# A two-block network on one Trainium2 core: the first mixer reordered, its rotation done by VectorE, and six modulation chunks summed by VectorE within the attention steps

## The reference, cut to what matters

```
mod = (silu(c) @ ada_w[layer] + ada_b[layer])      # 1024 -> 6144, for 2 layers
sh1, sc1, g1, sh2, sc2, g2 = split(mod, 6)
h = rms_norm(x, norm1_g) * (1 + sc1) + sh1
rq, rk, rv, rg, aq, ak, av = split(h @ w_in)       # 1024 -> 3584
rq, rk = rotary(rq), rotary(rk) * RET_DIM ** -0.5  # x1*cos - x2*sin, x1*sin + x2*cos
ret = head_rms(retention(rq, rk, rv)) * silu(rg)
att = chunk_attention(rms_norm(aq), rms_norm(ak), av, rel_bias)   # 8 heads of 64
x = x + g1 * (concat([ret, att]) @ w_out)
```

## Time and profile before

| | us |
|---|---|
| three runs, median | 1947.06 |
| profiled execution | 1949.58 |
| its span in the trace | 1947.8 |
| TensorE busy in it | 1744.1 |
| VectorE busy in it | 1256.5 |

### The profile page before, as it was taken

One profiled execution on the slowest core, in us unless ns is written; L12 is line 12 of the kernel. 1 busy time (PEld: TensorE's weight loads), 2 busy tenths in 40 slices (PEclk: granted clock), 3 DMA queues, 4 the chain that ended last, 5 costly groups with the idle time before them and its releaser, 6 DMA issues.

```text
span 1947.8 us, 26490 instructions
## 1 busy us (share of the span) xinstructions
PE 1744.1 (90%) x9260; PEld 1446.3 (74%) x9260; DVE 1256.5 (65%) x1990; ACT 1074.5 (55%) x1649; POOL 13.8 (1%) x29
## 2 busy tenths in 40 slices
PE   5898779999997998699999999977999897679998
PEld 4786367887884866687887678656999775569997
DVE  5675557889885846488898744755545555555454
ACT  2443237888874454488888643556444554554443
POOL 1000000000000000000000000000000000000000
PEclk9999879999998998799999999798999998879999
DMA  9875637999993945299999844121665552215652
GB/s 348 297 248 173 217 129 267 322 363 348 324 363 128 341 129 176 78 369 329 326 380 326 286 135 141 44 87 53 186 194 182 178 194 66 87 44 173 189 179 85
DMA packets 217282, 413.04 MB, mean 212 GB/s; under 512 B 13120, under 2 KB 69488, under 8 KB 216800
## 3 DMA queue, kind: packets, MB, share of 16 engines
q1 hardware_dynamic: 214176, 400.74, 59.9%
q0 software_dynamic: 1904, 8.26, 1.3%
q10 hardware_dynamic: 1120, 2.97, 0.4%
HBM read 410.87 MB, written 1.05 MB: 211 GB/s over the span
## 4 chain that ended last, share of the span: by engine, by line
PE 80%; DVE 10%; ACT 5%; issue 3%; DMA 2%; DVEq 0%; ACTq 0%; SPq 0%
PE banks L727 21%; PE banks L729 20%; PE banks L728 20%; DVE weights_low L2048 2%; PE banks L973 2%; PE banks L776 2%; PE banks L1058 2%; PE banks L1109 2%; PE banks L871 1%; DMA weight_ring<-in_ada_w 1%; DVE row_gains L2319 1%; PE banks L749 1%; ACT scratch L1648 1%; DMA weight_ring<-in_even_w_in 1%; ACT weights_high L1497 1%
## 5 line engine op out<-in xcount | busy, mean ns | idle before, releaser
L2048 DVE TENSOR_TENSOR weights_low<-weight_ring,weights_high 128x1024 fp32r<-128x1024 f32 (+1 forms) x656 | 771.8, 1218 | 199.1 <-ACT weights_high L1497 115.4
L727 PE MATMUL banks<-weights_high,features_parts 128*128 128x512 f32 (+1 forms) x1488 | 595.9, 400 | 30.0 <-DVE features_parts L2481 8.2
L728 PE MATMUL banks<-weights_low,features_parts 128*128 128x512 f32 (+1 forms) x1488 | 584.5, 393 | 0.0
L729 PE MATMUL banks<-weights_high,features_parts 128*128 128x512 f32 (+1 forms) x1488 | 584.5, 393 | 0.0
L1777 ACT ACTIVATE weights_high<-weight_ring 128x1024 fp32r<-128x1024 f32 x384 | 392.9, 1056 | 105.3 <-PE banks L729 73.4
L727 PEld LDWEIGHTS banks<-weights_high,features_parts 128*128 128x128 f32 x1488 | 284.0, 191 | 96.1 <-issue 20.3
L729 PEld LDWEIGHTS banks<-weights_high,features_parts 128*128 128x128 f32 x1488 | 282.8, 190 | 60.4
L728 PEld LDWEIGHTS banks<-weights_low,features_parts 128*128 128x128 f32 x1488 | 284.1, 191 | 56.1 <-issue 1.0
L1497 ACT ACTIVATE weights_high<-weight_ring 128x1024 fp32r<-128x1024 f32 (+1 forms) x176 | 176.6, 1043 | 149.6 <-PE banks L729 90.6
L727 PE MATMUL banks<-features_parts,weights_high 128*128 128x256 f32 x736 | 210.9, 287 | 0.2
L728 PE MATMUL banks<-features_parts,weights_high 128*128 128x256 f32 x736 | 208.6, 283 | 0.0
(11 more groups left out here) (373 smaller groups left out, 1611.1 us busy)
## 6 DMA issues: line engine op xcount, KB each, us to landing
weight_ring<-in_exp_w_gate SPq DMA_DIRECT2D x128, 512.0 KB, 5.1
weight_ring<-in_exp_w_up SPq DMA_DIRECT2D x128, 512.0 KB, 5.0
weight_ring<-in_exp_w_down SPq DMA_DIRECT2D x128, 512.0 KB, 5.2
weight_ring<-in_ada_w SPq DMA_DIRECT2D x96, 512.0 KB, 5.4
weight_ring<-in_ffn_wg SPq DMA_DIRECT2D x44, 512.0 KB, 4.1
weight_ring<-in_ffn_wu SPq DMA_DIRECT2D x44, 512.0 KB, 4.7
weight_ring<-in_ffn_wd SPq DMA_DIRECT2D x44, 512.0 KB, 4.1
weight_ring<-in_even_w_in SPq DMA_DIRECT2D x28, 512.0 KB, 5.6
```

The source lines that it names most:

```text
L727: eng.matmul(dst, lh, rh, start=first, stop=False, **kw)
L728: eng.matmul(dst, lh, rl, start=False, stop=False, **kw)
L729: mm = eng.matmul(dst, ll, rh, start=False, stop=last, **kw)
L2048: V(half_of(low(s), i, size), half_of(slot(n), i, size), half_of(high(s), i, size).bitcast(F32), ALU.subtract)\
```

## The change

The order of the modulation chunks moves. In the input projection six chunks are summed instead of four, at j = 0, 1, 3, 4, 5, 6 (chunks 4 to 9); none at j = 2. SyncE loads in that order. Chunks 10 to 15, four of which TensorE multiplied before, are all summed by VectorE, one in each `in_a0(t)` for t = 0 to 5, and each is handed over to TensorE and taken back within the same step, apart from the last, which TensorE sums over the partitions after the attention. The rotation is done in place by VectorE with `rotate` (for each block of tokens four products, a wait, a difference and a sum, a wait), and `turn_a0` then only transposes.

```diff
-ADA_EVEN, ADA_A0, ADA_ODD, ADA_A1 = 4, 8, 4, 4
-ADA_ON_PE = (10, 11, 12, 14)
-ADA_A0_ORDER = [8, 10, 9, 11, 12, 13, 14, 15]
+ADA_EVEN, ADA_A0, ADA_ODD, ADA_A1 = (0, 1, 3, 4, 5, 6), 6, 4, 4
+ADA_ON_PE = ()
@@ make_plan, and the same in the loads of SyncE
-        if j < ADA_EVEN:
+        if j in ADA_EVEN:
             ada(1)
@@ TensorE, turn_a0
-                        if x < 4:
-                            by_cos, by_sin = NB[:, tb, 128 * (2 * x + i):128 * (2 * x + i + 1)], turned_sin(tb, 2 * x + i)
-                            eng.matmul(dst, by_cos, ident, start=True, stop=False)
-                            mm = eng.matmul(dst, by_sin, ident, start=False, stop=True)
-                        else:
-                            mm = eng.transpose(dst, P0[:, tb, at + i * 128:at + (i + 1) * 128], ident)
+                        mm = eng.transpose(dst, P0[:, tb, at + i * 128:at + (i + 1) * 128], ident)
@@ TensorE, in_even
-                if 1 <= j <= ADA_EVEN:
+                if j in (1, 2, 4, 5):
                     modulation((2, 3))
@@ TensorE, after the retention values, and in_a0
             modulate_a0(0)
+            modulate_a0(1)
                 if t == 0:
-                    modulate_a0(1)
+                    modulate_a0(2)
                 if t == 1:
-                    modulate_a0(2)
+                    modulate_a0(3)
                     eng.wait_ge(a0_mixed, 1)
...
-                    modulate_a0(3)
                     features_wait(RET_HEADS)
-                if t == 2:
-                    modulate_a0(4)
-                if t == 3:
-                    modulate_a0(5)
-                    modulate_a0(6)
+                if 2 <= t <= 4:
+                    modulate_a0(t + 2)
             attention(Pairs("a0", P0), in_a0)
             modulate_a0(7)
@@ VectorE, in_even
-                if 1 <= j <= ADA_EVEN:
-                    ada_take(3 + j, (2, 3))
+                if j in (1, 2, 4, 5):
+                    ada_take((0, 4, 5, 0, 6, 7)[j], (2, 3))
                 if j == 2:
...
+                    tmp = [NB[:, i // 2, (i % 2) * 512:(i % 2 + 1) * 512].rearrange("p (h n) -> p h n", h=8) for i in range(4)]
                     for tb in range(TB):
...
-                    ins.then_inc(a0_rotated, 1)
+                        rotate(P0[:, tb, 0:1024].rearrange("p (h n) -> p h n", h=8), wide(cos_a[:, tb].unsqueeze(1), 128, 8, 64),
+                               wide(sin_a[:, tb].unsqueeze(1), 128, 8, 64), 64, tmp)
+                    eng.memset(FINI[:, :], 0.0).then_inc(a0_rotated, 1)
@@ VectorE, after the projection
-            ada_steps(KD)
             for h in range(RET_HEADS):
...
+            take_a0(0)
+            take_a0(1)
@@ VectorE, in_a0
                 if t == 0:
-                    ada_steps(KD)
                     root(8)
...
                     ins.then_inc(a0_mixed, 1)
+                    ada_steps(KD)
+                    take_a0(2)
                 if t == 1:
-                    for x in range(3):
-                        take_a0(x)
+                    ada_steps(KD)
...
+                    take_a0(3)
-                if t == 2:
-                    take_a0(3)
+                if 2 <= t <= 5:
                     ada_steps(KD)
-                if t in (3, 4):
-                    take_a0(t + 1)
+                    if t < 5:
+                        take_a0(t + 2)
                 if t == 5:
-                    ada_steps(KD)
-                    take_a0(6)
-                if t == 6:
                     take_a0(7)
```

More of the change, by code:

```diff
@@ L285, in a0_squares @@
             return PR[:, at:at + 512] if j == 2 else SCRF[:, 1536 + 512 * tb:2048 + 512 * tb]
-        def turned_sin(tb, h):
-            at = EVEN_IN * tb + (1024, 3072)[h // 4] + 128 * (h % 4)
-            return PR[:, at:at + 128]
         def pview(n):
@@ L858, in modulate_a0 @@
             def modulate_a0(x):
-                j, bank = ADA_A0_ORDER[x], 6 + x % 2
+                j, bank = 8 + x, 6 + x % 2
                 if x >= 2:
-                    eng.wait_ge(mod_taken, 4 + ADA_EVEN + x - 1)
+                    eng.wait_ge(mod_taken, 8 + x - 1)
                 if j not in ADA_ON_PE:
@@ L1187, in in_even @@
                         turn_a0(4 + x, 2048 + 256 * x)
-                    eng.wait_ge(mod_taken, 4 + ADA_EVEN)
+                    eng.wait_ge(mod_taken, 8)
                     eng.wait_ge(a0_taken, 4)
@@ L1219, in in_a0 @@
                             mm.then_inc(feature_turned, 2)
-                    modulate_a0(3)
                     features_wait(RET_HEADS)
-                if t == 2:
-                    modulate_a0(4)
-                if t == 3:
-                    modulate_a0(5)
-                    modulate_a0(6)
+                if 2 <= t <= 4:
+                    modulate_a0(t + 2)
             attention(Pairs("a0", P0), in_a0)
             modulate_a0(7)
-            ada[0] += ADA_A0
+            ada[0] += 2 + ADA_A0
             eng.wait_ge(mod_taken, 16)
@@ L2614, in in_even @@
                     ins.then_inc(a0_normed, 1)
-            project("even_in", tiles[st["even_in"][-1][0][1]]["split"] + 1, in_even, range(ADA_EVEN))
+            project("even_in", tiles[st["even_in"][-1][0][1]]["split"] + 1, in_even, ADA_EVEN)
             eng.wait_ge(more_loaded, MORE)
-            ada_steps(KD)
             for h in range(RET_HEADS):
@@ L2624, in take_a0 @@
             def take_a0(x):
-                ada_take(ADA_A0_ORDER[x], (6 + x % 2,), room)
+                ada_take(8 + x, (6 + x % 2,), room)
+            take_a0(0)
+            take_a0(1)
             def in_a0(t):
                 if t == 0:
-                    ada_steps(KD)
                     root(8)
```

## The result

The changed kernel took 1963.83 us (median of 4 runs, 1962.88 to 1963.96) against 1948.67 for the kernel before beside it (1945.42 to 1954.35): ratio 1.0064, 95% interval 1.0049 to 1.0079, so +12.5 us with +9.5 to +15.4. In five more rounds it was 1962.42 against 1949.98, 1.0060 [1.0047, 1.0074], +11.7 us. Differences are taken from these ratios throughout; the two medians of the first comparison lie 15.2 us apart, where the kernel before by itself spread over 9. One of the ten runs of e1, at 2912.55 us, was a slow one and is not in its ratio. The forecast was 1954.2, +7.1, and the range ended at 1959.5: the time lies outside it.

The account below looks back on a forecast made before the run. TensorE was taken to bound most of the kernel, with it and VectorE handing work to each other in the attention. Projection +0.4 and attention +6.7 made +7.1 on a median of 1947.06: 1954.2 us, range over the cases 1942.5 to 1959.5.

Parts of the forecast that it names:

- the main term: Attention: sums and hand-overs in series on VectorE and TensorE, mostly at half clock, add 6.7 us.
- (1): Rival, attention: TensorE's clock stays full, attention -3.0 us, total -2.6, 1944.5 us; chance 0.19.
- (2): Rival, projection: VectorE becomes its bound and the attention begins 4 us later; total +11, 1958 us; chance 0.14.
- (4): Rival, attention: full clock and hand-overs hidden behind TensorE's work on the heads; -10.7 us, 1936.4 us; chance 0.04.
- (3): Rival: all bursts at half clock and signals between engines longer than counted; +11.3 us, 1958.4 us; chance 0.11.
- the sum at half clock: Attention: sums, scaling, hand-overs, features and heads added in series come to 73.6 us, against 65.15 before, +8.4.
- Rotation: Input projection: twelve VectorE operations take 7.8 us and end at 116.0, 1.4 us later than before.
- Projection: 75 to 173 us: 0.5 us of gain left before group 6, 0.9 lost to one more hand-over burst; sum +0.4.
- the 0.7 given back: Projection, group 4: 0.7 us of its 2.1 us gain is lost to first matmuls at the half clock.
- Attention: 175.6 to 240.7 us: +8.4 us at half clock or -3.0 at full, taken as +6.7.
- 85%: Attention: the share taken of the difference between full and half clock, giving +6.7 us.
- its like would take 1956.7: Whole kernel: the profiled execution's 1949.58 us with the forecast 7.1 us added gives 1956.7.

Follow-up runs that it names:

- e1: The changed kernel, but in the attention each chunk's take and hand-over come one step after its sum; 1949.97 us, ratio 0.9980 to the kernel before.
- e7: The changed kernel with the old rotation, products by cos and sin added in PSUM by TensorE; 1959.49 us, ratio 1.0044 to the kernel before.
- e3: The changed kernel with 5 to 9 unread TensorE products ahead of each of six attention hand-overs; 1955.21 us, ratio 1.0016 to the kernel before.
- e2: The changed kernel with chunks 10, 11, 12 and 14 back on TensorE, 13 and 15 on VectorE; 1942.44 us, ratio 0.9953 to the kernel before.
- e12: The changed kernel with chunks 10, 11, 12, 14 back on TensorE, run again in five rounds; 1938.30 us, ratio 0.9944 to the kernel before.
- e9: The kernel before with two useless VectorE copies behind the attention, 1.42 us of delay; 1951.33 us, ratio 1.0005 to the kernel before.
- e6: The kernel before with only the rotation changed, in place on VectorE with plain transposes; 1949.66 us, ratio 0.9997 to the kernel before.
- e8: The changed kernel with chunks 10, 12, 14 on TensorE and 11, 13, 15 on VectorE, handed over late; 1947.82 us, ratio 0.9987 to the kernel before.
- e10: The kernel before with four useless VectorE copies behind the attention, 2.87 us of delay; 1951.33 us, ratio 1.0004 to the kernel before.
- e11: The kernel before with ten useless VectorE copies behind the attention, 7.24 us of delay, a repeat run; 1961.63 us, ratio 1.0053 to the kernel before.

## Why the prediction was wrong

**The direction and the main term were right.** Of the rivals none is what happened. The full clock (1) didn't come: 0.60 and bursts of 1.55 to 1.84. Attention did not begin 4 us late (2): its first pass ended 1.4 later. Hand-overs were not hidden (4). All bursts slow with longer signals (3) came nearest in the change, +11.3, and not for what happened: the stage took 71.9, less than the 73.6 of the sum at half clock.

**Rotation: right.** Twelve operations in 7.74 us, ending at 115.85 (forecast 7.8, 116.0):

```profile
108.11 2.48 DVE L2194 TENSOR_TENSOR normed<-projected,qk_features 128x512 f32<-128x512 f32 x4
110.63 0.69 DVE L2196 TENSOR_TENSOR projected<-normed 128x512 f32<-128x512 f32 x1
...
115.85 0.06 DVE L2577 MEMSET finisher<- 128x2 f32 x1
```

The four products take 2.48, starts 0.60 apart; the sum that waits for them starts 0.72 behind the last of them (110.63 - 109.91). So a wait does lengthen the pace here, by some 0.1. The section "The DRAIN you can't avoid" of the page "VectorE: DVE Perf Modes" of the Trainium skill has a semaphore behind each copy cost nothing extra; these rows don't agree with it.

**Projection: +1.4 where +0.4 was forecast.** Group 4 began at 128.65, 2.25 us earlier than in the earlier trace rows (forecast 128.8). But its first matmuls ran at the half clock for longer than the 0.7 given back: the hand-over behind group 4 came at 141.71, before at 141.91, so all but 0.2 was lost again.

```profile
127.03 1.97 PE L1144 MATMUL banks<-constants,projected 128*128 128x128 f32 x8 [7.75 <-ACT qk_features L1806]
...
128.65 0.77 PE L721 MATMUL banks<-weights_high,features_parts 128*128 128x512 f32 x1
...
132.63 0.60 PE L721 MATMUL banks<-weights_high,features_parts 128*128 128x512 f32 x1
133.06 0.40 PE L722 MATMUL banks<-weights_low,features_parts 128*128 128x512 f32 x1
...
141.71 0.95 PE L848 MATMUL banks<-constants,row_gains 128*128 128x1 f32 x8
...
153.54 0.95 PE L848 MATMUL banks<-constants,row_gains 128*128 128x1 f32 x8
...
173.12 1.84 PE L848 MATMUL banks<-constants,row_gains 128*128 128x1 f32 x16
```

From 128.65 to 133.06 ten products took 4.4 us; at the 0.23 to 0.24 of the later ones they take 2.35, so the start cost 2.1. Then come the new hand-over, 0.8 us more at 153.54, so that group 6 began at 158.07 (before 157.47, forecast 157.0), and the double one at 173.12 (+0.9, as forecast). The rotation's products taken from TensorE bought nothing: it stood 7.75 us in their place. In e7, with the products back, group 4 began at 130.89 and the hand-over behind it came at 141.87. The forecast's reading of VectorE's load there was wrong as well: the 16.85 us of the earlier trace rows already held some 5 us of chunk 8's sum (from 151.93), which it added once more to get 29. The window was 24.4 us busy, and rival 2, which leaned on the 29, had less behind it than it seemed.

**Attention: +6.8 in the two traces, +6.7 forecast.** Burst lengths and hand-overs came out nearly as listed, at 71.9 for 71.9 (65.15 + 6.7 = 71.85); the first sum began at 179.28 (forecast near 178). How near the total came is in part luck: 85% was chosen, not read. In the trace the heads of one step of four ran at the full clock, 2.7 us where the list has 4.4 at the half, and these 1.7 are what parts 71.9 from 73.6. e1 and e3 confirm the two mechanisms, each by itself: 12.5 us go with the series of hand-overs, 7.6 or more with the clock. DMA was no term, as said: no idle time of VectorE in this stage ends on a transfer.

**The step that failed** is how the number was carried from one trace to the time: "The output projection starts at the half clock in either kernel" and "its like would take 1956.7". The forecast took the stages behind as a fixed 1704.4 us and the old attention as a fixed 65.15, each read once. Neither is fixed, and the sum has no term for either: an equal clock at the first product was the only reason given. The miss of the time, 9.6 us, also holds 1.6 of the base: the kernel before has its median at 1948.67 beside the changed one, where three runs had given 1947.06.

Behind: the kernel before, by five draws, takes 1704.4 to 1711.2 us from the output projection on, mean 1707.6; its profiled execution was the shortest of the five, and of all fourteen. The changed kernel showed 1710.7 and 1710.2. That is +2.8 on the means, +6.2 in the pair. That one program varies so, without any shift, e2 and e12 show: 1709.4 and 1705.0.

The attention before: 65.1 in the profiled execution, 62.6 to 63.3 in four others. One chunk of sixteen products makes most of it, here in the trace of before and below in e9's:

```profile
193.49 8.73 PE L871 MATMUL banks<-weight_ring,c_features 128*128 128x512 f32 x16
```

```profile
193.25 7.03 PE L871 MATMUL banks<-weight_ring,c_features 128*128 128x512 f32 x16
```

The granted clock over these sixteen was 0.80 and 1.00. The mean of the five is 63.4, so by the means the change costs the stage 71.6 - 63.4 = 8.2, not 6.8.

The end of the first pass has a mean too, 174.3 in the five and 176.8 in the changed kernel's two: +2.5, of which 0.6 is there already at the first product of E0 (69.5 and 70.1), ahead of the change. With the means the sum is 2.5 + 8.2 + 2.8 = 13.5; the ratios gave 11.7 [9.2, 14.4] and 12.5 [9.5, 15.4]. It lies within both, but five and two draws don't make these means firm, and the +2.8 least of all: whether the changed kernel falls into the long form of the later stages more often than the one before, or did so by chance, stays open. The table leans to the first: the six kernels with the old order of chunks (e6 among them) have 1704.4 to 1711.2, mean 1707.6, the eight with the new one 1705.0 to 1715.3, mean 1710.6; e1 and e8, which start the output projection earlier than before, have the longest. e9 and e10 show that the long form needs nothing of the change; their medians (+1.0, +0.8) show that a small shift doesn't bring it every time. What a timetable could have had: the range. A stage behind that can take 39.3 or 41.0 us with the same instructions, and a stage ahead that can take 62.6 or 65.1, put by our estimate some 3 us on either side of any forecast from one trace; the range's upper end came from rivals alone, at 1959.5.

The Trainium skill, page "TensorE: Matmul & The Clock Gate", section "Part 1: The HAM clock gate (the "warmup" mystery)", says that the number of slow matmuls at a start differs from run to run of the same kernel. The rows agree: of the same 32 records at 26 us the first nine were slow in the trace of before and none in e11's. The forecast had read the page's other rule, "HAM oscillation", for the attention (all bursts cold, +8.4); the stage had one run of heads at the full clock in it, and measured +6.8.

## What to carry to other kernels

In a stage where two engines hand work to each other, giving one engine the work of the other adds it up in series and also takes from TensorE what held its clock: e1 prices the series at 12.5 us of a stage of 72, e3 the clock at 7.6, and e2, with four of the chunks on TensorE, is 19.6 shorter. If work has to move, put the hand-over a step behind the sum, and look for a stage where its new engine idles: chunk 9's sum went into the input projection in e2, which is the fastest kernel here, though e2 moved chunk 15 as well. Before adding up from one trace, look at the granted clock of the stages that the change leaves alone; each that lay between the two levels (0.82 in the attention, 0.84 and 0.83 behind it) came out otherwise in another run here, and the range has to hold that.

## What was not expected of the hardware

- Ahead of the change too the same code varied: 32 records at 26 us took 9.06 us in the trace of before and 7.18 in e11's. In the first the products start 0.43 apart up to the ninth and then 0.22, in the second 0.22 from the start, though the windows view gives a clock of 1.00 for both. That is 1.9 of the 3.7 us by which the end of the first score pass varied (172.0 to 175.7).
- From the output projection on the same instructions took 1704.4 to 1711.2 us behind the old attention and up to 1715.3 behind the others, in steps: over the fourteen traces the stretch of 152 TensorE records took 39.2 to 39.4 us at clock 0.83 or 40.9 to 41.1 at 0.79, and 41.5 once (0.75), and nothing between; the gather 9.2 to 9.6 or 10.6 to 10.8.
- The start of a long group at the half clock, behind a wait of 7.75 us, cost 2.1 us, nearly all of the 2.25 us by which the group had been brought forward.
- In e3, TensorE issued 74 records more than in the changed kernel within the stage (198 for 124) and the stage grew 7.6 us shorter.
